# Every fourth weight piece's low part subtracted on GpSimd in place of VectorE, in a two-layer decoder trunk

## What is computed

```python
x = layer_norm(x, ln_in_g, ln_in_b)
for l in range(2):
    hcat = x @ w_in[l]                      # 1024 x 6662: q, k, v of three attentions, forget gate, 3 x 1024 gates
    ya = forgetting_attention(...)          # 6 heads, decay from cumsum(log_sigmoid(f))
    yb = dilated_attention(rope(q), rope(k), v)   # 3 patterns x 4 heads
    yc = moba_attention(rope(q), rope(k), v)      # 6 heads
    merged = sig(g0) * (ya @ w_pa[l]) + sig(g1) * (yb @ w_pb[l]) + sig(g2) * (yc @ w_pc[l])
    x = layer_norm(ALPHA * x + merged @ w_o[l], ln1_g[l], ln1_b[l])
    hid = silu(x @ w_gate[l]) * (x @ w_up[l])     # 1024 x 2816 each
    x = layer_norm(ALPHA * x + hid @ w_down[l], ln2_g[l], ln2_b[l])
```

## Time and profile before

| | |
|---|---|
| Median of three runs | 906.3 us (905.82 to 906.94) |
| Span of the profiled execution, first to last instruction | 905.5 us |
| What lies around the span (median less span) | 0.8 us |
| TensorE busy | 869.5 us, 96% |
| VectorE busy | 534.9 us, 59% |
| ScalarE busy | 396.6 us, 44% |
| GpSimd busy | 52.0 us, 6% |
| VectorE's subtractions of weights, line 827 | 142, 307.4 us in all |
| Mean granted TensorE clock | 0.997 of full |
| DMA traffic | 149.34 MB, mean 165 GB/s |

### The profile page before, as it was taken

The page is one execution under the profiler, slowest core; times in us unless marked ns, Lnnn a source line. Parts: engine busy times, 40 slices in busy tenths (PEclk is TensorE's granted clock), DMA queues, the critical chain, the costliest instruction groups (busy, mean ns, idle before and its releaser), DMA issues.

```text
span 905.5 us, 10788 instructions
## 1 busy us (share of the span) xinstructions
PE 869.5 (96%) x4148; PEld 711.6 (79%) x4148; DVE 534.9 (59%) x814; ACT 396.6 (44%) x541; POOL 52.0 (6%) x100
## 2 busy tenths in 40 slices
PE   2999999999998999999999999999999899999995
PEld 1887787788887888888878788877888788888884
DVE  6575564646787545445685656555658855445436
ACT  3463445545434434444337444554543454344330
POOL 0011142000000000000000213300000000000000
PEclk9999999999999999999999999999999999999998
DMA  8572424256544855565436342333664575665601
GB/s 305 171 266 82 140 74 137 93 186 223 183 150 170 274 188 184 188 194 176 152 106 232 118 139 82 128 117 117 209 232 140 175 247 189 211 196 161 215 1 47
DMA packets 93314, 149.34 MB, mean 165 GB/s; under 512 B 3408, under 2 KB 52688, under 8 KB 93264
## 3 DMA queue, kind: packets, MB, share of 16 engines
q1 hardware_dynamic: 93264, 148.65, 50.2%
HBM read 147.59 MB, written 1.05 MB: 164 GB/s over the span
## 4 chain that ended last, share of the span: by engine, by line
PE 85%; DVE 7%; ACT 3%; DMA 2%; issue 2%; POOL 1%; SPq 0%; DVEq 0%; POOLq 0%
PE bank L1016 74%; PE bank L1079 4%; DVE w_lo L827 3%; PE bank L1031 2%; DMA raw<-in_w_in 2%; PE bank L1101 2%; ACT w_hi L745 1%; PE bank L1091 1%; PE bank L1041 1%; DVE stats L950 1%; DVE x L983 1%; DVE x L947 1%; DVE x L980 1%; DVE act_lo L832 0%; PE bank L1059 0%
## 5 line engine op out<-in xcount | busy, mean ns | idle before, releaser
L827 DVE TENSOR_TENSOR w_lo<-raw,w_hi 128x2048 fp32r<-128x2048 f32 (+3 forms) x142 | 307.4, 2168 | 93.6 <-ACT w_hi L745 93.3
L1016 PE MATMUL bank<-w_hi,act_hi 128*128 128x512 f32 (+2 forms) x864 | 343.0, 397 | 3.4 <-DVE act_lo L832 3.4
L1016 PE MATMUL bank<-w_hi,act_lo 128*128 128x512 f32 (+2 forms) x864 | 332.9, 385 | 0.0
L1016 PE MATMUL bank<-w_lo,act_hi 128*128 128x512 f32 (+2 forms) x864 | 332.2, 384 | 0.0
L745 ACT CAST w_hi<-raw 128x2048 fp32r<-128x2048 f32 (+3 forms) x142 | 257.1, 1812 | 131.6 <-PE bank L1016 102.1
L1016 PEld LDWEIGHTS bank<-w_hi,act_hi 128*128 128x128 f32 x864 | 162.8, 188 | 38.5 <-DVE act_lo L832 3.8
L1016 PEld LDWEIGHTS bank<-w_hi,act_lo 128*128 128x128 f32 x864 | 162.7, 188 | 33.0
L1016 PEld LDWEIGHTS bank<-w_lo,act_hi 128*128 128x128 f32 x864 | 163.2, 189 | 28.6
L1016 PE MATMUL bank<-w_hi,y_hi 128*128 128x512 f32 x240 | 95.2, 396 | 0.0
L1016 PE MATMUL bank<-w_hi,y_lo 128*128 128x512 f32 x240 | 93.6, 390 | 0.0
L1016 PE MATMUL bank<-w_lo,y_hi 128*128 128x512 f32 x240 | 93.5, 389 | 0.0
(11 more groups left out here) (86 smaller groups left out, 548.8 us busy)
## 6 DMA issues: line engine op xcount, KB each, us to landing
raw<-in_w_in SPq DMA_DIRECT2D x48, 1024.0 KB, 5.1
raw<-in_w_gate SPq DMA_DIRECT2D x44, 512.0 KB, 3.9
raw<-in_w_up SPq DMA_DIRECT2D x44, 512.0 KB, 4.9
raw<-in_w_down SPq DMA_DIRECT2D x22, 1024.0 KB, 4.9
raw<-in_w_o SPq DMA_DIRECT2D x8, 1024.0 KB, 5.0
raw<-in_w_in SPq DMA_DIRECT2D x4, 768.0 KB, 4.4
raw<-in_w_pa SPq DMA_DIRECT2D x4, 768.0 KB, 4.4
raw<-in_w_pc SPq DMA_DIRECT2D x4, 768.0 KB, 4.4
```

The source lines that it names most:

```text
L827: dve.tensor_tensor(weights(w_lo, i, HI_SLOTS), weights(raw, i, RAW_SLOTS), weights(w_hi, i, HI_SLOTS).bitcast(F32), ALU.subtract).then_in ...
L1016: ins = pe.matmul(bank[use[0]][:, 0:width], a, w[:, k, c0:c0 + width], start=start and k == 0 and p == 0, stop=stop and k == nk - 1 and p ...
```

## The change

Pieces 3, 7, 11 and so on (35 of the 142) have their low part subtracted by GpSimd. A new semaphore `pool_lo_done` counts the finished pieces of GpSimd, and `lo_done` now counts those of VectorE alone. Whoever waits for a low part (SyncE before it refills a slot of `raw`, TensorE before it multiplies) waits for the count that belongs to that piece. GpSimd's wait for the constant tables, which stood ahead of everything, now stands ahead of its first `rope` or `sum` step. The planner's list and all sizes stay as they are.

```diff
+POOL_EVERY = 4
+def on_pool(i):
+    return i % POOL_EVERY == POOL_EVERY - 1
+def pool_parts(i):
+    return (i + 1) // POOL_EVERY
...
+        pool_lo_done = sem("pool_lo_done")
...
+        def wait_lo(engine, i):
+            if on_pool(i):
+                engine.wait_ge(pool_lo_done, pool_parts(i))
+            else:
+                engine.wait_ge(lo_done, i + 1 - pool_parts(i))
...
                     if i >= RAW_SLOTS:
-                        sp.wait_ge(lo_done, i - RAW_SLOTS + 1)
+                        wait_lo(sp, i - RAW_SLOTS)
...
-            pool.wait_ge(tables_loaded, 32)
+            tables_here = False
             for step in PLAN:
+                if step[0] == "lo" and on_pool(step[1]):
+                    i = step[1]
+                    pool.wait_ge(hi_done, i + 1)
+                    pool.tensor_tensor(weights(w_lo, i, HI_SLOTS), weights(raw, i, RAW_SLOTS),
+                                       weights(w_hi, i, HI_SLOTS).bitcast(F32), ALU.subtract).then_inc(pool_lo_done, 1)
+                    continue
+                if not tables_here and step[0] in ("spread", "sum"):
+                    pool.wait_ge(tables_loaded, 32)
+                    tables_here = True
...
-                if kind == "lo":
+                if kind == "lo" and not on_pool(step[1]):
                     i = step[1]
                     dve.wait_ge(hi_done, i + 1)
...
-                    pe.wait_ge(lo_done, i + 1)
+                    wait_lo(pe, i)
```

## The result

The changed kernel takes 920.6 us in the median of four runs (919.49 to 921.81), the kernel before 906.06 us beside it; the ratio is 1.016 (95% interval 1.0145 to 1.0174). It is slower, as forecast, but by 14.5 us and not by 11.1, and the median lies 0.1 us above the top of the range. The profiled execution of after is the longest of the four, 921.81 us with a span of 919.9 us, against a span of 905.5 us before. Each execution on record takes 1.7 to 2.1 us more than its own span, so the profiled execution of before took some 907.3 us by this estimate, and not 906.3; the 0.8 us in the table of before compares two different executions. It cancels here, since both profiled executions are slow ones of their kernel: the spans differ by 14.4 us and the medians by 14.5.

The account below looks back on a forecast made before the run. The prediction took TensorE, busy 96% of the span, as the bound. Six terms, 2.25 + 1.7 + 1.6 + 0.4 + 1.2 + 3.95 = 11.1 us, gave 917.4 us, own range 915 to 920.5, and 909.5 to 920.5 for 8 in 10.

Parts of the forecast that it names:

- What bounds the kernel: Whole kernel: TensorE, busy 96% of the span, sets the time; none of the ten subtractions on the chain moves.
- the first rope: Layer 0's first chunk, near piece 11: the first rope step ends sooner, saving TensorE 0.36 us of idling.
- The price of the moved instruction: A full piece's subtraction takes 4.54 us on GpSimd, from a line through two smaller additions, against 2.29 on VectorE.
- The rivals with a fast or a slower GpSimd: GpSimd as fast as VectorE: 907.6 us, chance 0.05; at 5.83 us a piece: some 924, over 920.5 at 0.09.
- Where it costs nothing: Feed-forward part, 33 of a layer's 71 pieces: low parts are ready long before use, so the longer subtraction is hidden.
- Terms 2 to 6: Delays at piece 11 (second rope) +1.7, 79 (forget gate) +1.6, 7 +0.4, 39 (norm) +1.2, 107 (merge) +3.95 us.
- term 5: Piece 39 before the norm: GpSimd's subtraction makes VectorE start piece 40 late, +1.2 us.
- Term 1: Piece 3 at the start: TensorE waits for the longer subtraction, with no lead, +2.25 us.
- The hold of VectorE: Pieces 79, 7, 39 and 107: a VectorE instruction with two SBUF inputs waits until GpSimd's ends.
- the rival that VectorE isn't held: No hold of VectorE: only terms 1 and 2 are left, 3.95 us, giving 910.3 us; chance 0.14.
- the rival of the lost race at piece 107: VectorE's merge starts before GpSimd's piece 107: 0.55 us there, not 3.95, giving 914.0 us; chance 0.25.
- Whatever makes it wait longer is added to the span nearly in full.: Whole kernel: TensorE sets the time, so any longer wait of TensorE lengthens the span by nearly that much.

Follow-up runs that it names:

- ffn_only: Changed kernel with only twelve full pieces in the two feed-forward stretches on GpSimd, the rest on VectorE; 906.51 us, ratio to before 1.0001.
- chunks: Changed kernel with each GpSimd subtraction cut into four instructions of a quarter of the columns; 918.00 us, ratio to before 1.0133.
- chosen_6: Changed kernel with only pieces 41, 42, 74, 75, 112 and 113 on GpSimd; 910.33 us, ratio to before 1.0044.
- only_107: Changed kernel with only piece 107 on GpSimd; 911.64 us, ratio to before 1.0055.
- filler_all: Changed kernel with extra unused matmuls ahead of seven TensorE waits, 63 in all; 917.43 us, ratio to before 1.0119.
- filler: Changed kernel with 12 extra unused matmuls before the wait for piece 3 and 14 before layer 1's first merge; 918.68 us, ratio to before 1.0134.
- only_3: Changed kernel with only piece 3 on GpSimd; 909.13 us over ten runs, ratio to before 1.0035.
- no_3_107: Changed kernel with pieces 3 and 107 back on VectorE; 911.77 us, ratio to before 1.0063.

## Why the prediction came out as it did, step by step

**What bounds the kernel** was right, and that the change shortens nothing on the chain: no step of after is a gain but the -0.55 us of the first rope, which the forecast had as -0.36.

**The price of the moved instruction** was right: 4.54 us against 4.53 to 4.63. The straight line through the earlier trace rows held for a size eight times that of its larger row. The rivals with a fast or a slower GpSimd are out.

**Where it costs nothing** was right, shown by ffn_only for the pieces away from the norms. The 77 us that were to leave VectorE were 76, but 25 of them came back as longer instructions.

**Terms 2 to 6** were right to 0.2 us (table above). In term 5 the way differed a little: GpSimd slipped in between two scalings, and what it held was the second of them (5.11 us in place of 0.75), not piece 40; the end of it was the same.

**Term 1** was sized by durations alone. GpSimd's longer duration is +2.25 us; in after 0.5 us came on top because the transfer was later (the casts begin at 26.22 and not at 25.73), and in two other runs, where it came earlier, the term was 1.32 and 1.60. The range of this term, 1.3 to 2.9 us, was missing.

**The hold of VectorE** (terms 3 to 6) was the step for which no row stood. It is there, in full length, shown by chunks and chosen_6: an instruction of VectorE waited 4.1 us for a whole subtraction, 0.9 us for a quarter, and 1.1 us for the subtraction of a small piece. The rule of the Trainium skill that the prediction named (page "SBUF — State Buffer", section "SBUF: two separate sides") says that whichever of the two starts first has the shared ports for its whole instruction. The traces agree in both directions: GpSimd's piece 41 took 5.53 us, since it waited first for VectorE's piece 40, and VectorE's instruction on one number a partition took 4.45 us; the rival that VectorE isn't held is out, and so is the rival of the lost race at piece 107 (0.29 us of lead in after, the same in only_107).

**The step that failed is the one at the beginning: "Whatever makes it wait longer is added to the span nearly in full."** It is added in full, and then the granted clock can fall behind the wait. The sum had no term for this; it left it at nothing without a reason. Behind the stalls of 2.84 and 3.56 us seven matmuls each started 0.43 us behind the one before them, and one or two more a little late, which cost 1.56 and 1.58 us, together 3.1 of the 3.4 us by which the sum fell short (the rest is the third fall and the 0.2 us of the six terms, less 0.16 us at the start). The trace of before had no such case to read it from: once its clock is up, no stall there is longer than 1.64 us, and no fall follows one. filler_all shows that it is TensorE's standing still and not GpSimd's work: the same subtractions, the same waits, no idle TensorE at these places, no fall, 917.43 us. A third fall, behind 2.69 us in the norm, lost 1.58 us and got 1.38 of them back, since TensorE had idled 0.70 and 0.26 us there in the kernel before, for VectorE:

```profile
282.17 0.44 PE L1031 MATMUL bank<-tables,act_fn 128*128 128x128 f32 x2 [0.70 <-DVE act_fn L935]
282.86 0.63 PE L1031 MATMUL bank<-tables,x 128*128 128x128 f32 x4 [0.26 <-DVE act_lo L832]
```

That the first measurement lies 0.1 us above the range and the second, 919.35 us, inside it is chance; the missing term is in both.

In the ten traces of experiments, that of after and that of before (each one's stall of 3.2 to 3.4 us at the very start, where the matmuls are still 0.43 us apart, left out), the clock fell behind 12 of 13 stalls of 2.2 us and more, and behind 3 of 33 of 1.2 to 2.1 us. One of 3.23 us (in chunks) went without a fall, and one of 1.47 us (in filler) had one. (The Trainium skill, page "TensorE: Matmul & The Clock Gate", section "The HAM clock gate (the "warmup" mystery)", says that the number of slow matmuls at the start of one kernel varies from run to run. It says so of the start; further on the two traces of after agree with it: behind stalls of 2.69 and 2.67 us in the norm, six steps of 0.43 us in one and four in the other.) Which of the stalls between these are hit, and whether one can be made safe other than by work for TensorE, stays open. That the spread of the times of one kernel comes from the falls is shown in part. Each measurement has only one trace, but every run's mean granted clock is on record. In filler, chunks and only_3 the longest run has the lowest clock (920.69 us at 0.991 against 918.45 to 918.77 at 0.993 and 0.994; 920.00 at 0.990 against 917.92 to 918.02 at 0.993; 912.34 at 0.994), and filler_all, without falls, stays within 1.0 us. In after the runs at 0.993 took 918.19 to 919.68 us and those at 0.991 919.13 to 921.81, which overlap, and in no_3_107 two runs at 0.996 lie 2.5 us apart, so the falls are not the whole of it; the transfers of the start vary too.

## What to carry to other kernels

Work that moves from VectorE to GpSimd is not taken away from VectorE's time: for as long as GpSimd's instruction ran, an instruction of VectorE with two inputs from SBUF waited for its end in every case looked at here, however small it was (4.45 us in place of 0.16). So look at what VectorE does during the 4.5 us of each moved instruction, and move those whose old place is right ahead of something for which TensorE waits, if GpSimd is done by then: three of them gave 5.7 us, where thirty-five lost 14.5.

When a long stall of TensorE is forecast (2.2 us and more here), its price is its length and, in 12 of 13 cases here, more for the matmuls behind it, 1.2 to 1.7 us (2.4 us once), unless slack is there to take them up.

## What the runs showed of the hardware

- Matmuls of 512 columns started 0.43 us apart behind long stalls and 0.23 us apart otherwise, for 4 to 9 matmuls each time; 12 and 14 matmuls with unused results, issued into the two longest stalls, prevented it, and the step at the merge stayed 3.8 us.
- A VectorE instruction on 128x1 numbers took 4.45 us in place of 0.16 while GpSimd subtracted; `act_lo`, with one input in a PSUM bank, ran its normal 1.29 us for two inside another such subtraction.
- GpSimd's subtraction takes 4.54 us for 2048 numbers a partition in one instruction, and 5.4 us in four.
